# A fused transformer layer on one Trainium2 core: when the second half's tokens are loaded, squared and transposed, and how the last output tile is stored

## The reference, cut to what matters

```python
mod_x = jnp.split((jax.nn.silu(c) @ w_ada[l] + b_ada[l])[:, None, :], 6, axis=-1)
mod_c = jnp.split((jax.nn.silu(c_ctx) @ w_ada[l] + b_ada[l])[None, None, :], 6, axis=-1)
...
hc = modulate(xc, norm_g[l, 0], mod_c[0], mod_c[1])       # rms_norm(x, g) * (1 + scale) + shift
h = modulate(x, norm_g[l, 0], mod_x[0], mod_x[1])
qa, ka, va, u, qw, kw, vw, gate = split_mixer_inputs(h @ w_in[l])
...
x = x + mod_x[5] * rms_norm(swiglu(h2, w_ffn_in[l], w_ffn_out[l]), norm_g[l, 3])
```

## Time and profile before

| | before |
|---|---|
| device time, median of 3 runs | 1778.73 us (1776.87 to 1779.0) |
| profiled execution: its own time | 1778.41 us |
| profiled execution: span | 1776.4 us |
| TensorE busy | 1737.5 us, 98% |
| VectorE busy | 1222.7 us, 69% |
| ScalarE busy | 804.2 us, 45% |
| GpSimd busy | 766.7 us, 43% |
| mean granted TensorE clock | 0.996 of full speed |

### The profile page before, as it was taken

One profiled execution on the slowest core, in us unless ns is written; L12 is line 12 of the kernel. 1 busy time (PEld: TensorE's weight loads), 2 busy tenths in 40 slices (PEclk: granted clock), 3 DMA queues, 4 the chain that ended last, 5 costly groups with the idle time before them and its releaser, 6 DMA issues. The chain is left out here.

```text
span 1776.4 us, 25757 instructions
## 1 busy us (share of the span) xinstructions
PE 1737.5 (98%) x9180; PEld 1479.4 (83%) x9180; DVE 1222.7 (69%) x1719; ACT 804.2 (45%) x1576; POOL 766.7 (43%) x494
## 2 busy tenths in 40 slices
PE   8999999999998999999999999899999999999998
PEld 6997888888887999899988878778888888888886
DVE  3528688879958999778843366875666566576766
ACT  3525333434637888656520145633333333344453
POOL 1407677776633899420022242465555555400000
PEclk9999999999999999999999999999999999999999
DMA  8333333445767665512034242233223323386734
GB/s 329 106 103 123 115 119 143 156 153 182 265 172 210 170 146 137 151 33 72 1 143 160 89 166 84 83 106 120 94 94 127 121 94 128 114 278 208 253 102 177
DMA packets 98375, 249.86 MB, mean 141 GB/s; under 512 B 12257, under 2 KB 25953, under 8 KB 98146
## 3 DMA queue, kind: packets, MB, share of 16 engines
q1 hardware_dynamic: 98274, 248.52, 41.9%
HBM read 183.07 MB, written 65.41 MB: 140 GB/s over the span
## 5 line engine op out<-in xcount | busy, mean ns | idle before, releaser
L736 POOL TENSOR_TENSOR ring<-raw_w,ring 128x512 fp32r<-128x512 f32 x120 | 186.9, 1575 | 139.9 <-ACT ring L607 139.8
L78 PE MATMUL psum<-h_hi,ring 128*128 128x512 f32 x400 | 156.8, 392 | 3.0 <-ACT z L653 2.0
L80 PE MATMUL psum<-h_hi,ring 128*128 128x512 f32 x400 | 156.4, 391 | 0.0
L79 PE MATMUL psum<-h_lo,ring 128*128 128x512 f32 x400 | 156.2, 391 | 0.0
L78 PE MATMUL psum<-u_slot 128*128 128x512 f32 x308 | 120.5, 391 | 0.9 <-DVE u_slot L2933 0.7
L80 PE MATMUL psum<-u_slot 128*128 128x512 f32 x308 | 120.2, 390 | 0.0
L79 PE MATMUL psum<-u_slot 128*128 128x512 f32 x308 | 119.9, 389 | 0.0
L607 ACT ACTIVATE ring<-raw_w 128x512 fp32r<-128x512 f32 x120 | 72.5, 625 | 101.0 <-DVE raw_w L895 32.3
L1386 DVE TENSOR_REDUCE mx<-psum 128x1 f32<-128x1280 f32 x64 | 95.1, 1486 | 6.8 <-PE psum L1272 6.0
L1319 ACT ACTIVATE e<-psum,neg_m 128x1280 f32<-128x1280 f32 x64 | 85.0, 1328 | 31.2 <-DVE neg_m L1387 31.2
L2532 POOL TENSOR_TENSOR cut_lo<-i_raw,cut_hi 128x512 fp32r<-128x512 f32 x44 | 66.8, 1520 | 59.2 <-ACT cut_hi L2387 59.2
(11 more groups left out here) (412 smaller groups left out, 5219.0 us busy)
## 6 DMA issues: line engine op xcount, KB each, us to landing
raw_w<-in_w_pairs SPq DMA_DIRECT2D x40, 512.0 KB, 4.6
qk_dram<-room SPq DMA_DIRECT2D x26, 512.0 KB, 3.6
room<-in_w_ada SPq DMA_DIRECT2D x24, 512.0 KB, 5.4
gates_dram<-ost SPq DMA_DIRECT2D x24, 512.0 KB, 3.0
b_g<-gates_dram SPq DMA_DIRECT2D x8, 1536.0 KB, 7.5
stage<-in_w_ff SPq DMA_DIRECT2D x22, 512.0 KB, 5.9
i_raw<-in_w_ff SPq DMA_DIRECT2D x22, 512.0 KB, 4.8
f_dram<-h SPq DMA_DIRECT2D x22, 512.0 KB, 3.3
```

What stands on the lines that cost most here:

```text
L78: pe.matmul(out, sh, mh, start=first, stop=False, skip_group_check=onto)
L79: pe.matmul(out, sh, ml, start=False, stop=False, skip_group_check=onto)
L80: return pe.matmul(out, sl, mh, start=False, stop=last, skip_group_check=onto)
L736: pool.tensor_tensor(w_lo[i], source(p, i), w_hi[i].bitcast(F32), ALU.subtract).then_inc(w_lo_ready, 1)
```

## The change

Five edits in `mixer_in` and one in `ffn_out`. (1) The fourth token tile of the first half is asked for after `ada[11]` and no longer ahead of it (`TOKENS_BEHIND`). (2) The second half's tokens come as four transfers, each as soon as the `ada` tile under it is used. (3) ScalarE squares them between the modulations of units 4 to 7 instead of after them, and VectorE forms the mean ahead of the last `v_weight_lo`. (4) ScalarE takes one root of two numbers early, so that the table for roots is loaded then. (5) The transposes of units 0 and 1 stand one product later, those of unit 2 behind all products. (6) The last output tile is finished and stored in two halves of 128x512.

```diff
@@ -199,7 +199,7 @@
         ss, rs = sb("ss", [P, TT]), sb("rs", [P, TT])
 
 
-        small_in, x_in = sem("in_small"), {c: sem(f"in_x{c}") for c in (1, 2)}
+        small_in, ctx_in, x1_in = sem("in_small"), sem("in_ctx"), [sem(f"in_x1_{j}") for j in range(4)]
         cond_in = sem("in_cond")
         x0_in = wv_in = late_in = [sem(f"in_x0_wv_late{t}") for t in range(4)]
         ada_in = kw_in = [sem(f"in_ada_kw{j}") for j in range(ADA_BUFS)]
@@ -207,7 +207,7 @@
         sq_done, mean_ready, rs_ready, xn_ready = sem("in_sq"), sem("in_mean"), sem("in_rs"), sem("in_xn")
         turned, full_ready, hi_ready, dve = sem("in_turned"), sem("in_full"), sem("in_hi"), sem("in_dve")
         lo_ready = [sem(f"in_lo{j}") for j in range(2)]
-        lam_dots, lam_exp = sem("in_lam_dots"), sem("in_lam_exp")
+        lam_dots, lam_exp, table_ready = sem("in_lam_dots"), sem("in_lam_exp"), sem("in_root_table")
         vh_ready = [sem(f"in_vh{j}") for j in range(2)]
         vl_ready, v_done, v_copied = sem("in_vl"), sem("in_v_done"), sem("in_v_copied")
         v_out = [sem(f"in_v_out{j}") for j in range(2)]
@@ -260,6 +260,8 @@
             n, j = divmod(rt - 1, 2)
             return n + 4 * j if n < 4 else 8 + 2 * (n - 4) + j
 
+
+        TOKENS_BEHIND = (7, 8, 9, 11)
 
         @block.sync
         def _(sp):
@@ -275,16 +277,17 @@
                                      (sub_g[:], io["sub_g"])):
                         sp.dma_start(dst, src).then_inc(small_in, 16)
                     sp.dma_start(spare[:, 0:4 * HD], io["da_lambda"].to_broadcast([P, 4 * HD])).then_inc(small_in, 16)
-                if i in (7, 8, 9, 10):
-                    t = i - 7
+                if i in TOKENS_BEHIND:
+                    t = TOKENS_BEHIND.index(i)
                     sp.dma_start(xt[0][:, t, :], xv[:, t, :]).then_inc(x0_in[t], 16)
             for j in range(4):
                 sp.wait_ge(x0_in[j], 16)
                 sp.dma_start(v_raw[:, 2 * j:2 * j + 2, :], io["w_v"][:, 2 * j:2 * j + 2, :]).then_inc(wv_in[j], 16)
-            sp.wait_ge(ada_used, ADA)
-            sp.dma_start(xt[1][:], xv[:, 4:8, :]).then_inc(x_in[1], 16)
+            for j in range(4):
+                sp.wait_ge(ada_used, ADA - 3 + j)
+                sp.dma_start(xt[1][:, j, :], xv[:, 4 + j, :]).then_inc(x1_in[j], 16)
             sp.wait_ge(turned, 8)
-            sp.dma_start(xt[2][:, 0:2, :], cv).then_inc(x_in[2], 16)
+            sp.dma_start(xt[2][:, 0:2, :], cv).then_inc(ctx_in, 16)
 
             def store_v(t):
                 sp.wait_ge(v_copied, 2 * t + 2)
@@ -395,7 +398,7 @@
                     mm = pe.transpose(row_bank(k)[:, 2 * P + 2 * j:2 * P + 2 * j + 2], rows[:, k % 2, j * P:(j + 1) * P], ident[0:2, 0:2])
                 mm.then_inc(row_turned, 1)
 
-            BETWEEN = {13: 0, 14: 1, 15: 2}
+            BETWEEN = {14: 0, 15: 1}
             pe.wait_ge(silu_ready, 1)
             for k in range(KC):
                 if k >= 4:
@@ -412,8 +415,9 @@
                     pe.wait_ge(small_in, 80)
                 if k:
                     turn_rows(k - 1)
+            transposes(2)
+            turn_rows(KC - 1)
             transposes(3)
-            turn_rows(KC - 1)
 
             def value(t, k):
                 tok = slice(t * P, (t + 1) * P)
@@ -494,16 +498,16 @@
 
         @block.scalar
         def _(act):
-            def statistics(c):
+            def square(t):
+                c = t // 4
+                j = t - CH[c][0]
+                act.wait_ge(*((x0_in[j], 16), (x1_in[j], 16), (ctx_in, 16))[c])
+                if t:
+                    act.wait_ge(sq_done, t)
+                act.activation(junk, xt[c][:, j, :], ACT.Square, accum_out=ss[:, t:t + 1]).then_inc(sq_done, 1)
+
+            def root(c):
                 a, b = CH[c][0], CH[c][-1] + 1
-                if c:
-                    act.wait_ge(x_in[c], 16)
-                for t in CH[c]:
-                    if c == 0:
-                        act.wait_ge(x0_in[t], 16)
-                    if t:
-                        act.wait_ge(sq_done, t)
-                    act.activation(junk, xt[c][:, t - a, :], ACT.Square, accum_out=ss[:, t:t + 1]).then_inc(sq_done, 1)
                 act.wait_ge(mean_ready, c + 1)
                 act.activation(rs[:, a:b], ss[:, a:b], ACT.Sqrt).then_inc(rs_ready, 1)
 
@@ -555,21 +559,32 @@
             act.activation(econd[:], cond[:], ACT.Exp, scale=-1.0).then_inc(e_ready, 1)
             act.wait_ge(lam_dots, 1)
             act.activation(lamd[:, 2:4], lamd[:, 0:2], ACT.Exp).then_inc(lam_exp, 1)
+            act.wait_ge(lam_exp, 1)
+            act.activation(rs[:, 0:2], lamd[:, 2:4], ACT.Sqrt).then_inc(table_ready, 1)
+            act.wait_ge(table_ready, 1)
             def v_weight_hi(k):
                 act.wait_ge(wv_in[k // 2], 32)
                 act.activation(v_hi[:, k, :], v_raw[:, k, :], ACT.Copy).then_inc(vh_ready[0], 1)
 
-            statistics(0)
+            for t in CH[0]:
+                square(t)
+            root(0)
             modulate(0)
             modulate(1)
             for u in range(2, 6):
                 v_weight_hi(2 * (u - 2))
                 modulate(u)
+                if u >= 4:
+                    square(u)
             modulate(6)
+            square(6)
+            square(7)
             modulate(7)
-            statistics(1)
+            root(1)
             values(0)
-            statistics(2)
+            for t in CH[2]:
+                square(t)
+            root(2)
             values(1)
             modulate(8)
             modulate(9)
@@ -797,10 +812,13 @@
                 v.tensor_scalar(A[:, k, :], ps[:, 2:4], scale_b[:, k:k + 1], norm_g[:, 0, k:k + 1], ALU.add, ALU.mult)\
                  .then_inc(ab_ready, 1)
 
-            def statistics(c):
+            def mean(c):
                 a, b = CH[c][0], CH[c][-1] + 1
                 v.wait_ge(sq_done, b)
                 v.tensor_scalar(ss[:, a:b], ss[:, a:b], 1.0 / D, EPS, ALU.mult, ALU.add).then_inc(mean_ready, 1)
+
+            def normalise(c):
+                a, b = CH[c][0], CH[c][-1] + 1
                 v.wait_ge(rs_ready, c + 1)
                 ch.link(v.reciprocal(rs[:, a:b], rs[:, a:b]))
                 for t in CH[c]:
@@ -848,7 +866,8 @@
             for k in range(4):
                 copy_rows(k + 1)
                 modulation(k)
-            statistics(0)
+            mean(0)
+            normalise(0)
             copy_rows(5)
             modulation(4)
             unit(0)
@@ -864,9 +883,11 @@
             for k in range(3, KC):
                 unit(k)
                 v_weight_lo(k - 1)
+            mean(1)
             v_weight_lo(7)
-            statistics(1)
-            statistics(2)
+            normalise(1)
+            mean(2)
+            normalise(2)
             for u in range(8, 16):
                 unit(u)
             k_weight_lo(0)
@@ -2972,6 +2993,7 @@
     X, Y = banks[0:T], banks[T:2 * T]
     left, right = (lambda rows, t: rows[:, t, 0:HALF]), (lambda rows, t: rows[:, t, HALF:D])
     row_of = lambda n: io["out"][n * P:(n + 1) * P, :]
+    LAST_PARTS = (slice(HALF, D), slice(0, HALF))
 
     @block.sync
     def _(sp):
@@ -2991,10 +3013,13 @@
             sp.wait_ge(out_ready, t + 1)
             sp.dma_start(row_of(t), low[:, t, :]).then_inc(stored, 16)
             sp.dma_start(x[t][:], io["x_mid"][T + t]).then_inc(x_in[t], 16)
-        for t in range(T):
+        for t in range(T - 1):
             sp.wait_ge(y_ready, T + t + 1)
             sp.dma_start(row_of(T + t), high[:, t, :]).then_inc(stored, 16)
-        sp.wait_ge(stored, 16 * 2 * T)
+        for n, part in enumerate(LAST_PARTS):
+            sp.wait_ge(y_ready, 2 * T + n)
+            sp.dma_start(row_of(2 * T - 1)[:, part], high[:, T - 1, part]).then_inc(stored, 16)
+        sp.wait_ge(stored, 16 * (2 * T + 1))
 
     @block.tensor
     def _(pe):
@@ -3146,8 +3171,9 @@
             ch.link(v.reciprocal(one, one))
             v.wait_ge(weighed, T + t + 1)
             v.wait_ge(x_in[t], 32)
-            v.scalar_tensor_tensor(out=high[:, t, :], in0=high[:, t, :], scalar=one, in1=x[t][:], op0=ALU.mult, op1=ALU.add)\
-             .then_inc(y_ready, 1)
+            for part in (LAST_PARTS if t == T - 1 else (slice(0, D),)):
+                v.scalar_tensor_tensor(out=high[:, t, part], in0=high[:, t, part], scalar=one, in1=x[t][:, part], op0=ALU.mult, op1=ALU.add)\
+                 .then_inc(y_ready, 1)
 
 
 def tables():
```

## The result

The changed kernel takes 1782.64 us (median of 14 runs, 1777.11 to 1787.12), the kernel before 1778.87 us in the runs beside it (14 runs, 1775.34 to 1781.55): a ratio of 1.0022, 95% interval 1.0014 to 1.0030. It is slower by 3.8 us, above the range that was given. All 26 together have a mean of 1781.5 us with a standard error of 0.5, against 1778.7 with 0.2 for 112 runs of before: 2.8 us is the better figure for the loss, and 3.8 holds some chance. (Ratios here go by medians; the differences that the experiments add up go by means.)

What follows compares the result with a forecast made beforehand. TensorE, busy 98% of the span, was taken as the bound. Begin +0.1, store -0.6 and clock +1.7 us gave +1.2 on 1778.41, so 1779.6, stated as 1779.5, range 1776.0 to 1781.2.

Steps and rivals of the forecast that it cites:

- The sum: Whole kernel: begin +0.1, store -0.6 and clock +1.7 us make +1.2 on 1778.41, so 1779.6, stated as 1779.5.
- The fourth token tile behind `ada[11]`: Begin: `ada[11]` lands 1.27 us earlier, so TensorE's 0.56 us wait goes; the token tile lands 1.27 us later.
- The early table: Begin, ScalarE and VectorE: early root-table load takes 1.08 us off the chain from mean to scaling, costing nothing where moved.
- Units 0 and 1 one product later: Begin: tokens are ready before TensorE reaches unit 0's transposes, so the wait there goes, -0.43 us.
- Unit 2 behind all products: Begin: last `turn_rows` comes 3.2 us after unit 2's transposes, with 2.6 us idle; first value product +1.15 us.
- Squares between modulations: Begin, ScalarE: unit 7's modulation comes some 0.8 us late, but the wait ahead of unit 8 goes, -0.73 us.
- rival D: Begin: ScalarE bounds between modulations, unit 8's gain is lost and the clock falls; +4.4 us, 1782.8, chance 0.07.
- The last tile in halves: End of the span: first half's data move while the second half is made and issued, -0.6 us.
- The clock: Behind the new 2.6 us TensorE wait in the begin, the granted clock may fall, costing up to 1.7 us.
- forecast A: Whole kernel: as summed, the clock falls behind the new TensorE wait; 1779.5 us, chance 0.50.
- three of three: Argument that the clock falls: it fell behind each of the three earlier TensorE waits of 2.0 us or more.
- B: Whole kernel: same new wait, but the clock holds; +0.1 - 0.6, 1777.9 us, chance 0.27.

Runs made afterwards that it cites:

- e2: The changed kernel unchanged, run again with a second profile: median 1780.76 us, ratio 1.0008 to the kernel before.
- e5: The kernel before plus six small copies of one number on ScalarE where it is idle: median 1780.65 us, ratio 1.0009.
- e6: e3's kernel plus eight small copies on ScalarE: median 1777.51 us, ratio 0.9994 to the kernel before.
- e3: The changed kernel with the transposes of units 0 to 2 back in their old places: median 1778.10 us, ratio 0.9996 to the kernel before.
- e9: e7's kernel plus eight small copies on ScalarE: median 1775.89 us, ratio 0.9989 to the kernel before.
- e7: The changed kernel with VectorE's copy_rows(7), modulation(6) and modulation(7) ahead of unit(2): median 1778.53 us, ratio 0.9995 to the kernel before.
- e10: The changed kernel plus eight small copies on ScalarE, nothing else: median 1778.18 us, ratio 0.9998 to the kernel before.
- e1: The kernel before, unchanged, run again against itself: median 1778.83 us, ratio 0.9999.
- e11: The kernel before with only the transposes of units 0 to 2 moved as in the change: median 1780.77 us, ratio 1.0013.
- e12: The kernel before with only the last tile finished and stored in two halves, executed once: 1776.56 us.
- e4: The changed kernel with VectorE's copy_rows(7) moved directly behind unit(1): median 1780.77 us, ratio 1.0005 to the kernel before.
- e8: The changed kernel with ten wasted 128x128 products in TensorE's wait ahead of the last turn_rows: median 1780.70 us, ratio 1.0007 to the kernel before.

## Why the prediction was wrong

The forecast was wrong: 1782.64 lies above 1781.2, the top of its range, and slower by over 0.2% had a chance of 0.07. The 26 runs together, with a median of 1781.7 and a mean of 1781.5, still lie above it.

**What failed is a cost put at nothing.** "The sum" was made of the begin, the store and the clock. It has no term for ScalarE's longer program (of the early table it says "it costs nothing there"), and it took for granted that a program whose work is unchanged between 60 and 1770 us takes the same time there. It does not. Six ScalarE instructions more, whatever they do, put a fetch into the start of the late weights' transfers, where ScalarE and TensorE have next to no slack (a TensorE wait of 0.2 us before): 2.5 to 4.0 us in six of seven traces, nothing in the seventh (e2), about 2 us in the mean times. Adding them alone costs 2.1 us (e5); taking the fetch out of that place gives back 1.3 (e6 against e3), 1.9 (e9 against e7) and 2.3 to 3.2 us (e10), each with an error of 0.7 to 0.8. No rival named it. The prediction's own test, "if the wait is under 1 us, if waits appear among value products, if the span behind the last matmul has not shrunk", looked only where the diff is.

**Nearly everything in the begin came as worked out.** *The fourth token tile behind `ada[11]`*: the 0.56 us wait is gone. But it is 0.48 in e1 and absent in e5, e11 and e12, which have the old order too, and the changed kernel now waits 0.34 us one product earlier, so this gain is not shown to be the edit's. *The early table*: 1.08 us worked out, 1.08 measured. The table's load itself took 1.28 us, where the page "ScalarE: Activation LUTs" in the Trainium skill (section "What ACT_TABLE_LOAD costs") adds 1.4 us of drain: with the load gone the chain got shorter by 1.08 us, so no trace here shows the drain. *Units 0 and 1 one product later*: no wait; e3 and e6, with the old place, have 0.51 and 1.33 us there. *Unit 2 behind all products*: 3.2 us from the transposes to the last `turn_rows`, 3.28 measured; 2.6 us of idle time, 2.63 measured. *Squares between modulations*: unit 7's modulation 0.8 us late, 0.76 measured (unit 7's transposes at 51.54, its modulation at 52.94, 1.40 after; before 0.64 after them), and the wait ahead of unit 8 gone: rival D did not come, and that its 1782.8 is nearly the measured time is chance. The begin together was put at +0.1 us; from `ada[10]`'s product to unit 8's transposes it is 33.65 us against 33.86 (25.30 to 59.16): -0.2. The four traces with the old begin (before, e1, e5, e12) take 33.0 to 33.9, in the mean 33.5, and against that it is +0.1. The stretch does not tell the two apart.

**The last tile in halves**: 0.6 forecast, 0.4 to 0.45 measured (e12 alone, and both traces of the changed kernel). The landing came 0.58 us sooner, as forecast (2.61 to 2.03 us); the second VectorE instruction was put at +0.05, and from the start of VectorE's last work to the last issue it is 0.13 us more (1.32 to 1.45). The 2.0 us that the prediction quotes from the Trainium skill's page "DMA: Bandwidth & Descriptors" (section "Anatomy of one DMA") stand there for transfers issued by GpSimd. These stores are SyncE's, and 2.61 less 1.27 us of data leaves 1.3, 2.03 less 0.64 leaves 1.4.

**The clock**: forecast A took it to fall, for 1.7 us, because it had fallen behind all three waits of the earlier trace rows. That was one execution. The 2.0 us wait near 163 us stands in all 14 traces, and the clock falls behind it in four (before, e3, e6, e7). In e1, the same program as before, it holds, with 27 matmuls where the earlier trace rows have 21 in as long a stretch:

```profile
164.00:170.00 6.00, 6.00 (x27) 4.98 (x28) 4.73 (x6) 3.81 (x7) 4.93 (x4) 1.00 0.01 3
```

Between 100 and 200 us e1 took 1.6 us less, which confirms the price of 1.7. So the price was right and the step "three of three" was too strong: behind the new wait the clock fell in one trace of four. In the mean, the changed kernel's granted clock is 0.9952, with an error of 0.0003, against 0.9960. 0.0008 of 1780 us is 1.4 us of lost clock, but some of that stands near 446 us, behind the late tile's wait, and cannot be told apart. e11's 3.0 us against 1.3 us of direct cost (e3 against e2) leaves 1.7 for the clock. e10's 0.0 leaves 0.3 to 0.6, with begin and store taken off. With an error of 0.7 on each, the size stays open: between B and A.

**The books.** Begin -0.2 to +0.1, store -0.4, and +2.1 for the fetch with the clock falls behind it (e5): +1.5 to +1.8, where 26 runs say +2.8 with 0.5 of error. The 1.0 to 1.3 left over is what the clock behind the new wait may have taken; it was not measured there. Without the fetch, e10 measured 0.0: within 0.2% as forecast, and between B and A. What the change's own work loses, it loses by edit 5, which alone costs the kernel before 3.0 us (e11): with it undone (e3 against before) or its chain broken (e7) the change is level, even with the fetch in its bad place.

Open: why a fetch of 8 KB beside some 3 MB of transfers makes them land up to 2.7 us late in the changed kernel. The runs show when it happens and that moving the fetch ends it; e2, with the fetch 0.1 us behind the issue and no wait, shows that it does not happen every time. Also open is whether other fetches, which moved too, cost anything.

## What to carry to other kernels

Before putting a transpose behind the last piece of work, look at what the next engine does between it and the thing that the following instruction waits for, and at the second thing behind that: e4 freed the first and gained nothing. When a change adds instructions to an engine's program, the work behind it may run otherwise; add the same number of idle instructions to the kernel before, and time that too, before looking for the cause in the work. Where runs of one kernel spread over 5 us, a difference of 2 to 3 needs a dozen runs or more of each (error 0.6 to 0.8), and one pair of traces proves only waits, not times. Read a fall of the clock from several executions before it is counted on.

## What the runs showed of the hardware

- A program's length moves its instruction fetches: six instructions on ScalarE moved an 8 KB fetch from 2.7 us to 0.1 us behind an issue, and with it the kernel's mean time by 2.1 us (e5). In the seven traces with the fetch 0.1 to 0.4 us behind the issue, the stretch around the waiting matmul was 2.5 to 4.0 us longer in six.
- TensorE's first products go at half pace, 6 or 7 in a microsecond. They begin at 4.6 to 5.2 us in all 14 traces, but the pace rises to 11 or 12 at 7.8 us in before, at 8.7 to 10.8 us in the others. `ada[10]`'s product begins at 25.3 us in before and at 25.4 to 26.9 in the others. About 1 us of a single execution's time is settled there, and the one trace that the forecast was made from was the earliest.
- The same 2.6 us wait left the clock at 1.00 in three executions and halved it for 6.8 us in a fourth. With ten products in the wait (e8) it held in the one profiled, which proves little beside those three. The 2.0 us wait near 163 us halved it for 3.4 us in 4 of 14.
